# Head gates of a recurrent block from high and low parts in three passes instead of fp32 products

## The reference

```python
def _rg_lru_terms(u, wa, ba, wx, bx, lam):          # u (B,T,1024), wa, wx (8,128,128)
    uh = u.reshape(bsz, n, RG_HEADS, RG_BLOCK)
    r = sigmoid(einsum("bthi,hij->bthj", uh, wa) + ba)
    i = sigmoid(einsum("bthi,hij->bthj", uh, wx) + bx)
    log_a = -RG_C * r * softplus(-lam)
    return exp(log_a), sqrt(-expm1(2.0 * log_a)) * (i * u)

# branches: z = h @ w_in; g, rec = halves of z; u = depthwise conv of 4 taps over rec; gelu(g)
# per direction: context scanned first, latent scan starts from its final state
# out = (gelu(g) * (scan forward + scan backward)) @ w_out
```

## Time and profile before

| | us |
|---|---|
| median of 3 runs (lowest, highest) | 2131.16 (2128.59, 2137.18) |
| the profiled execution | 2134.52 |
| its span | 2132.8 |
| PE, DVE, ACT, POOL busy | 2053.1, 1519.2, 831.5, 1292.4 |
| L752, gate products, records in the span | 192, from 88.9 to 345.2 |
| `u` ready in heads 0, 1, 2 and 7 | 88.9, 125.2, 159.9, 336.4 |

### The profile page before, as it was taken

How to read it: one execution, slowest core, us unless ns; L and a number is a source line. 1 busy time by engine, 2 the same in 40 slices (tenths; PEclk the granted TensorE clock), 3 DMA queues, 4 the chain that set the end, 5 groups by cost and what they waited for, 6 DMA issues and landing times. The chain is left out here.

```text
span 2132.8 us, 26628 instructions
## 1 busy us (share of the span) xinstructions
PE 2053.1 (96%) x9048; PEld 1661.6 (78%) x9048; DVE 1519.2 (71%) x1518; ACT 831.5 (39%) x1111; POOL 1292.4 (61%) x836
## 2 busy tenths in 40 slices
PE   6999999999999999999999999799999999999996
PEld 6677776878888888888888779678888888888885
DVE  7588889878777777777777674696655665566557
ACT  4666667447222232323222355463232223222322
POOL 4533234656877787787778352367765576557653
PEclk9999999999999999999999988899999999999998
DMA  8132322431222222222221400211111111111114
GB/s 306 69 119 71 121 75 88 192 139 60 80 89 89 88 79 89 89 73 86 91 89 65 168 30 11 89 51 68 49 49 49 59 49 49 49 59 49 49 40 158
DMA packets 55932, 179.68 MB, mean 84 GB/s; under 512 B 5041, under 2 KB 6353, under 8 KB 55249
## 3 DMA queue, kind: packets, MB, share of 16 engines
q1 hardware_dynamic: 55888, 179.13, 24.2%
HBM read 166.52 MB, written 12.58 MB: 84 GB/s over the span
## 5 line engine op out<-in xcount | busy, mean ns | idle before, releaser
L2089 DVE TENSOR_TENSOR Y<-Y,ps 128x1024 f32<-128x1024 f32 x336 | 409.9, 1221 | 53.8 <-PE ps L584 13.8
L1693 POOL TENSOR_TENSOR F_lo<-S,F_hi 128x1024 fp32r<-128x1024 f32 x44 | 107.1, 2434 | 351.5 <-ACT F_hi L1354 351.5
L584 PE MATMUL ps<-F_hi,WC_hi 128*128 128x512 f32 x736 | 231.7, 392 | 1.1 <-ACT Y L1392 1.1
L1329 ACT ACTIVATE S<-S 128x1024 f32<-128x1024 f32 x48 | 50.9, 1060 | 464.6 <-DVE S L2193 464.6
L584 PE MATMUL ps<-F_hi,WC_lo 128*128 128x512 f32 x736 | 230.5, 391 | 0.0
L1112 ACT ACTIVATE So_hi<-So_raw 128x512 fp32r<-128x512 f32 x132 | 82.7, 628 | 369.3 <-POOL So_raw L1567 365.7
L584 PE MATMUL ps<-F_lo,WC_hi 128*128 128x512 f32 x704 | 217.4, 390 | 0.0
L1671 POOL TENSOR_TENSOR So_lo<-So_raw,So_hi 128x512 fp32r<-128x512 f32 x132 | 188.4, 1453 | 5.8 <-ACT So_hi L1112 5.8
L584 PEld LDWEIGHTS ps<-F_hi,WC_hi 128*128 128x128 f32 x736 | 138.7, 189 | 31.3 <-ACT Y L1392 1.7
L584 PEld LDWEIGHTS ps<-F_hi,WC_lo 128*128 128x128 f32 x736 | 138.7, 188 | 29.2
L584 PEld LDWEIGHTS ps<-F_lo,WC_hi 128*128 128x128 f32 x704 | 132.4, 188 | 28.1
(11 more groups left out here) (302 smaller groups left out, 5381.1 us busy)
## 6 DMA issues: line engine op xcount, KB each, us to landing
rawA<-wA SPq DMA_DIRECT2D x62, 512.0 KB, 3.3
rawB<-wB SPq DMA_DIRECT2D x62, 512.0 KB, 3.3
E<-ada SPq DMA_DIRECT2D x46, 512.0 KB, 3.3
rawC<-wC SPq DMA_DIRECT2D x46, 512.0 KB, 3.6
quad<-ada SPq DMA_DIRECT2D x8, 2048.0 KB, 9.4
ada_first<-ada SPq DMA_DIRECT2D x4, 2048.0 KB, 16.1
outT<-X SPq DMA_DIRECT2D x16, 512.0 KB, 3.4
X<-outT SPq DMA_DIRECT2D x16, 512.0 KB, 7.0
```

What stands on the lines that cost most here:

```text
L584: mm = pe.matmul(out, w[:, w_cols:w_cols + P], (hi, lo)[part], start=first and w is W_hi[s] and part == 0, stop=last and w is W_lo[s])
L1329: A(S[0][:], S[0][:], ACT.Gelu_apprx_tanh).then_inc(gelu_done, 1)
L1693: TT(dst[:], S[1][:], F_hi[:].bitcast(F32), ALU.subtract).then_inc(f_ready, 1)
L2089: TT(Y[:, m], Y[:, m], flat(ps[:, b:b + 2, :]), ALU.add).then_inc(d_added, 1)
```

## The change

`gw` and `u` are split into high and low parts. ScalarE rounds `u` behind the convolution (`u_hi_ctx`, and the latent tokens into `F_lo`, a tile of a later stage that is free here); GpSimd makes `u_lo_ctx` and `u_lo` from them, and this now stands ahead of WA_lo in its order. ScalarE rounds the next head's `gw` between the next B weights and tanh (`round_gates`); GpSimd makes `gw_lo` as the last of its head. TensorE makes each gate in three passes (low x low is left out) in an order in which the first three passes need no low part of `u`. The load of the next `gw` no longer waits for the gates, but for `gw_lo`. Six semaphores of the context norm become one, with steps (the order of that work stays). `rec` starts 24 bytes later, so that `u_lo_ctx` can lie on it once the convolution has read it.

```diff
-        rec, u, RA0, Hc_hi, Hc_lo, RA1, IB0, IB1, TH0, TH1, gw = overlay(
-            64, ("rec", [P, TA + 3]), ("u", [P, TA]), ("RA0", [P, TA]), 1.25,
+        rec_pad, u, RA0, u_hi_ctx, Hc_hi, Hc_lo, RA1, IB0, IB1, TH0, TH1, gw, gw_hi, gw_lo = overlay(
+            64, ("rec", [P, TA + 9]), ("u", [P, TA]), ("RA0", [P, TA]), ("u_hi_ctx", [P, NC_], F32R), 0.125,
...
+        rec = rec_pad[:, 6:TA + 9]
+        u_lo_ctx, = overlay(64 + 1 / 32, ("u_lo_ctx", [P, NC_], F32R))
@@ SyncE, head_loads
-                    sp_.wait_ge(gate_done, 4 * hd + 4)
+                    sp_.wait_ge(gw_ready, hd + 1)
                     sp_.dma_start(gw[:], gatew[hd + 1]).then_inc(gw_full, 16)
@@ TensorE, head
-                pe.wait_ge(gw_full, 16 * hd + 16)
-                pe.wait_ge(u_made, hd + 1)
-                for gi in range(4):
...
-                    for out, src in ((ps[:, b, 0:NC_], u[:, 0:NC_]), (ps[:, b + 1], u[:, LAT:LAT + HF]),
-                                     (ps[:, b + 2], u[:, LAT + HF:TA])):
-                        mm = pe.matmul(out, gw[:, gi], src, start=True, stop=True)
-                    mm.then_inc(gate_done, 1)
+                pe.wait_ge(gw_ready, hd + 1)
+                pe.wait_ge(u_hi_made, hd + 1)
+
+                def gate_pass(gi, n):
+                    b = 3 * (gi % 2)
+                    w = gw_lo if n == 1 else gw_hi
+                    parts = (u_lo_ctx, u_lo) if n == 2 else (u_hi_ctx, F_lo)
+                    for out, src in ((ps[:, b, 0:NC_], parts[0][:]), (ps[:, b + 1], parts[1][:, 0:HF]),
+                                     (ps[:, b + 2], parts[1][:, HF:T])):
+                        mm = pe.matmul(out, w[:, gi], src, start=n == 0, stop=n == 2)
+                    return mm
+
+                for gi, n in ((0, 0), (0, 1), (1, 0), (0, 2), (1, 1), (1, 2), (2, 0), (2, 1), (2, 2), (3, 0), (3, 1), (3, 2)):
...
+                    if (gi, n) == (0, 2):
+                        pe.wait_ge(u_ready, hd + 1)
+                    if gi > 1 and n == 0:
                         pe.wait_ge(gate_evac, 4 * hd + gi - 1)
+                    mm = gate_pass(gi, n)
+                    if n == 2:
+                        mm.then_inc(gate_done, 1)
@@ ScalarE, head: behind round_hi("A", hd + 1)
+                act.wait_ge(u_made, hd + 1)
+                A(u_hi_ctx[:], u[:, 0:NC_], ACT.Copy)
+                A(F_lo[:], u[:, LAT:TA], ACT.Copy).then_inc(u_hi_made, 1)
@@ ScalarE, head: ahead of tanh
                 round_hi("B", hd + 1)
+                if not last:
+                    round_gates(hd + 1)
...
+            def round_gates(hd):
+                act.wait_ge(gw_full, 16 * hd + 16)
+                if not (isinstance(hd, int) and hd == 0):
+                    act.wait_ge(gate_done, 4 * hd)
+                A(gw_hi[:], gw[:], ACT.Copy).then_inc(gw_hi_made, 1)
@@ GpSimd
+            def lo_of_gates(hd):
+                pool.wait_ge(gw_hi_made, hd + 1)
+                TT(gw_lo[:], gw[:], gw_hi[:].bitcast(F32), ALU.subtract).then_inc(gw_ready, 1)
+
             def head(hd, last=False):
+                pool.wait_ge(u_hi_made, hd + 1)
+                TT(u_lo_ctx[:], u[:, 0:NC_], u_hi_ctx[:].bitcast(F32), ALU.subtract)
+                TT(u_lo[:], u[:, LAT:TA], F_lo[:].bitcast(F32), ALU.subtract).then_inc(u_ready, 1)
                 lo_of_unit("A", hd + 1)
-                pool.wait_ge(u_made, hd + 1)
...
                     lo_of_unit("B", hd + 1)
+                    lo_of_gates(hd + 1)
```

More of the change, by code:

```diff
@@ L98, in build_trunk @@
         W_lo = {"A": sb("WA_lo", [P, D], F32R), "B": sb("WB_lo", [P, D], F32R), "C": WC_lo}
+        u_lo, = overlay(("u_lo", [P, T], F32R))
         S = [sb("S0", [P, T]), S1]
@@ L123, in build_trunk @@
             ("ada_first", [P, ADA0, D]), ("ctx_x", [P, KT, NC_]), ("ctx_sq", [P, KT, NC_]), ("diag_c", [P, 2, P]))
-        rec, u, RA0, Hc_hi, Hc_lo, RA1, IB0, IB1, TH0, TH1, gw = overlay(
-            64, ("rec", [P, TA + 3]), ("u", [P, TA]), ("RA0", [P, TA]), 1.25,
+        rec_pad, u, RA0, u_hi_ctx, Hc_hi, Hc_lo, RA1, IB0, IB1, TH0, TH1, gw, gw_hi, gw_lo = overlay(
+            64, ("rec", [P, TA + 9]), ("u", [P, TA]), ("RA0", [P, TA]), ("u_hi_ctx", [P, NC_], F32R), 0.125,
             ("Hc_hi", [P, KT, NC_], F32R), ("Hc_lo", [P, KT, NC_], F32R), ("RA1", [P, TA]),
-            ("IB0", [P, TA]), ("IB1", [P, TA]), ("TH0", [P, TA]), ("TH1", [P, TA]), ("gw", [P, 4, P]))
+            ("IB0", [P, TA]), ("IB1", [P, TA]), ("TH0", [P, TA]), ("TH1", [P, TA]), ("gw", [P, 4, P]),
+            ("gw_hi", [P, 4, P], F32R), ("gw_lo", [P, 4, P], F32R))
+        rec = rec_pad[:, 6:TA + 9]
+        u_lo_ctx, = overlay(64 + 1 / 32, ("u_lo_ctx", [P, NC_], F32R))
         RA, IB, TH = (RA0, RA1), (IB0, IB1), (TH0, TH1)
@@ L244, in build_trunk @@
         rstd_made, rb_done = ([sem(f"{n}{h}") for h in range(2)] for n in ("rstd_made", "rb_done"))
-        csq_made, cssq_done, crms_made = sem("ctx_sq_made"), sem("ctx_ssq_done"), sem("ctx_rms_made")
-        crstd_made, cdiag_made, crb_done = sem("ctx_rstd_made"), sem("ctx_diag_made"), sem("ctx_rb_done")
+        ctx_step = sem("ctx_step")
+        CTX = {name: n + 1 for n, name in enumerate(("squares", "sum", "columns", "root", "inverse", "diagonal", "spread"))}
+        gw_hi_made, gw_ready, u_hi_made, u_ready = sem("gw_hi"), sem("gw_ready"), sem("u_hi"), sem("u_ready")
         cscaled, caffine, chi, hc_ready = sem("ctx_scaled"), sem("ctx_affine"), sem("ctx_hi"), sem("ctx_h_ready")
@@ L714, in _ @@
             ada_tile(0)
-            pe.wait_ge(csq_made, 2)
+            pe.wait_ge(ctx_step, CTX["sum"])
             for t in range(2):
                 mm = pe.matmul(ps[:, 0, t:t + 1], diag_c[:, t], ones[:, 0:1], start=True, stop=True)
-            mm.then_inc(cssq_done, 1)
+            mm.then_inc(ctx_step, 1)
             for n in range(1, 4):
                 ada_tile(n)
-            pe.wait_ge(cdiag_made, 1)
-            pe.matmul(ps[:, 3, 0:NC_], ones[:], diag_c[:], start=True, stop=True).then_inc(crb_done, 1)
+            pe.wait_ge(ctx_step, CTX["diagonal"])
+            pe.matmul(ps[:, 3, 0:NC_], ones[:], diag_c[:], start=True, stop=True).then_inc(ctx_step, 1)
             part_columns(16, 4, 4, 0)
@@ L739, in head @@
                     unit("B", hd, AB67)
-                pe.wait_ge(gw_full, 16 * hd + 16)
-                pe.wait_ge(u_made, hd + 1)
-                for gi in range(4):
-                    if gi == 0:
+                pe.wait_ge(gw_ready, hd + 1)
[9 more added lines that the diff above has]
+                for gi, n in ((0, 0), (0, 1), (1, 0), (0, 2), (1, 1), (1, 2), (2, 0), (2, 1), (2, 2), (3, 0), (3, 1), (3, 2)):
+                    if (gi, n) == (0, 0):
                         pe.wait_ge(rec_evac, hd + 1)
-                    elif gi == 1:
+                    if (gi, n) == (1, 0):
                         pe.wait_ge(ada_added, hd + 1)
-                    else:
+                    if (gi, n) == (0, 2):
+                        pe.wait_ge(u_ready, hd + 1)
+                    if gi > 1 and n == 0:
                         pe.wait_ge(gate_evac, 4 * hd + gi - 1)
-                    b = 3 * (gi % 2)
-                    for out, src in ((ps[:, b, 0:NC_], u[:, 0:NC_]), (ps[:, b + 1], u[:, LAT:LAT + HF]),
-                                     (ps[:, b + 2], u[:, LAT + HF:TA])):
-                        mm = pe.matmul(out, gw[:, gi], src, start=True, stop=True)
-                    mm.then_inc(gate_done, 1)
+                    mm = gate_pass(gi, n)
+                    if n == 2:
+                        mm.then_inc(gate_done, 1)
                 if not last:
@@ L1159, in _ @@
             act.wait_ge(ctx_full, 16)
-            A(ctx_sq[:], ctx_x[:], ACT.Square).then_inc(csq_made, 1)
+            A(ctx_sq[:], ctx_x[:], ACT.Square).then_inc(ctx_step, 1)
             act.wait_ge(memset_done, 3)
-            act.wait_ge(cssq_done, 1)
-            A(rms_c[:], ps[:, 0, 0:2], ACT.Sqrt, scale=1.0 / D, bias=eps[:, 0:1]).then_inc(crms_made, 1)
+            act.wait_ge(ctx_step, CTX["columns"])
+            A(rms_c[:], ps[:, 0, 0:2], ACT.Sqrt, scale=1.0 / D, bias=eps[:, 0:1]).then_inc(ctx_step, 1)
             for m in range(KT):
@@ L1237, in head @@
                     act.preload_act_table(ACT.Sqrt)
+            def round_gates(hd):
[3 more added lines that the diff above has]
+                A(gw_hi[:], gw[:], ACT.Copy).then_inc(gw_hi_made, 1)
             act.wait_ge(lam_ready, 1)
             act.wait_ge(zeros_ready, 1)
+            round_gates(0)
             head(0)
@@ L1626, in head @@
                     lo_of_unit("B", hd + 1)
-            pool.wait_ge(u_made, 1)
+                    lo_of_gates(hd + 1)
+            lo_of_gates(0)
             head(0)
@@ L1933, in _ @@
             TT(pbs[:], col("pool_b", 0, 8), col("pool_scale", 0, 8), ALU.mult)
-            dve.wait_ge(csq_made, 1)
+            dve.wait_ge(ctx_step, CTX["squares"])
```

(12 more changed lines are left out.)

## The result

| | before | changed |
|---|---|---|
| median (lowest, highest), 5 runs each | 2133.02 (2128.59, 2137.18) | 2152.17 (2148.19, 2158.75) |
| the profiled execution, its span | 2134.52, 2132.8 | 2158.75, 2156.8 |
| ratio to before | | 1.0098, 95% interval 1.0073 to 1.0124 |
| `u` ready, heads 1 to 7 | 125.2, 159.9, 195.2, 230.5, 265.8, 301.1, 336.4 | 126.2, 163.1, 202.6, 242.2, 279.4, 318.9, 358.4 |

The kernel is 19 us slower (16 to 26 by the interval), forecast 18. The profiled execution is the slowest of the five; between the two traces lie 24 us, and all of them come from the heads: +22.1 at the last `u`, +24.7 at the first norm behind them (the reciprocal at 408.6 against 433.4), +24.0 at the last norm of the kernel (2117.6 against 2141.6).

What follows compares the result with a forecast made beforehand. Two rings of almost the same length were taken to close each head, with `u` having about 0.5 us of slack. +12 us at the last `u`, +4.3 last head and +2 clock made +18 on 2131.2: 2149 us, range 2130 to 2163.

Steps and rivals of the forecast that it cites:

- What bounds the loop: Head loop: two dependency cycles of almost the same length close each head, leaving `u` about 0.5 us of slack.
- the two rings: Head-loop cycles from gate products to sqrt: one returns through Gelu and B unit, one through VectorE's scan and convolution.
- Part 1: TensorE's gate products: three passes take 7.0 us for four gates instead of 8.58, 1.6 us less a head.
- Part 2: Rounding and subtraction ahead of the gates: low parts ready at +5.8, last sigmoid at 12.35 instead of 9.66, +2.7 us.
- Part 3: Rounding the gate weights on ScalarE between B's rounding and tanh: +0.5 us, tanh at 15.2.
- Part 4: WA_lo moved from beside the convolution: its first instruction takes 0.95 instead of 2.96 us, -2.0 us every head.
- Part 5: VectorE alternating with GpSimd: `Y*TH` to 18.5, ada quad to 24.95, late by 0.6 us, its idle time gone.
- The sqrt would allow the next product at 24.4: VectorE's next product in a loop head: 21.16 plus 2.7 for sigmoids and 0.5 for gate weights.
- The clock: TensorE's clock drops behind a new 2 to 2.7 us gate stop: one head in four, +2 us, bounds 0 and 10.
- Hand-overs: Switches of the shared read path between GpSimd and VectorE: no price in the rows; at about 115 ns each, 2156.
- Last head: Low parts of the gated tokens behind the last `u`: VectorE comes to them late by the same alternation, +4.3 us.
- the ring: The closed chain of dependent instructions that sets a head's length, gate products through sigmoids, tanh and sqrt back to gate products.

Runs made afterwards that it cites:

- e7: Kernel before with one line moved: GpSimd waits for `u` before WA_lo, gates still fp32; 2134.9 us, ratio 1.0011.
- e1: Changed kernel with the sum of the two scans put into `rec`, so tanh waits for that sum and not `Y*TH`; 2141.98 us, ratio 1.0046.
- e4: Changed kernel with 12 extra 512-column products on TensorE in front of the wait for Gelu, to hold the clock up; 2161.16 us, ratio 1.0135.
- e5: Changed kernel with VectorE instead of GpSimd making the low parts of `u`; 2148.05 us, ratio 1.0074.
- e6: Changed kernel with VectorE making the low parts of `u` and the scans' sum put into `rec`; 2140.74 us, ratio 1.0026.
- e9: Changed kernel: VectorE makes `u`'s low parts, scan sum in `rec`, `Y*TH` behind next head's ada quad, extra weights ahead of head 0; 2133.83 us, ratio 1.0008.
- e8: Changed kernel without the low part of `u` and the third gate pass, scans' sum in `rec`; 2127.11 us, ratio 0.9966.
- e2: Changed kernel without the low part of `u` and the third pass of each gate; 2139.58 us, ratio 1.0033.

## Why the prediction came out right, and where it was wrong

- *What bounds the loop:* right for the kernel before. `u` had next to no slack, and what was put behind it was paid. e7 shows the two rings: 2 us off the convolution alone leave the head at 35.3.
- *Part 1:* the pass rate held (12 passes in the pattern of unit A, 0.58 apart). None of the 1.6 us came back in the changed kernel, and what they are worth when nothing waits is not measured.
- *Part 2:* right to 0.4 us. Low parts +5.4 (5.8 forecast), GpSimd's first piece got in ahead of VectorE's IB product, u_lo 3.25 us in record. Where the low parts hold the gates (e1, heads 2 and 5), the last sigmoid comes at +12.0 (12.35); the +12.5 of the head above agrees by luck, for there the late B unit held them.
- *Part 3:* right, +0.5 and nothing else; tanh at +14.8 in e1 (15.2).
- *Part 4:* the 2.0 us came (0.93 instead of 2.96). That WA_lo costs nothing in its new place was right for TensorE and wrong for VectorE, where part 5 charged it.
- *Part 5:* its times were right: `Y*TH` ended at +18.1 (18.5), the quad at +24.45 (24.95). **The step that failed is "The sqrt would allow the next product at 24.4".** It added the delays of the sigmoids and the weights to tanh and did not ask what else tanh waits for. I had `Y*TH` end at 18.5 and tanh begin at 15.2 in one text, and tanh overwrites what `Y*TH` reads. Before, `Y*TH` ended at 206.43, 0.7 ahead of tanh (207.17): a wait with a cover of 0.7 us, which no view of waits lists. The product came at +27.5, a long head is 39.5 and not 37.05. e1 takes this wait away and lands at 36.41.
- *The clock:* it fell where I put it in one head only. The gates' stop for the low parts was forecast at 2 us and more in each head; it was 1.97 us in head 1 of the changed kernel, and there the clock fell (0.69 from 132 to 134, 0.50 from 134 to 136), with the last sigmoid 0.85 us later than in e1. In later heads the stop was 0.8 us or none, 1.1 in e1. In the four long heads the clock fell behind the 3.7 us in front of the B unit, which follow from the tanh wait. By e4 these falls cost a long head nothing, where I had put in 2 us; the one in head 1 even made the head short (36.98 us against 39.52 in e4), because GpSimd's second IB product (+14.4) came behind `Y*TH` (+14.15).
- *Hand-overs:* right, they have no price in the rows. `Y*TH` ends 1.08 us behind the product that held it up, and takes 1.23 where nothing does (head 1 of the changed kernel).
- *Last head:* +2.6 (24.7 - 22.1) against 4.3.

So 19 against 18 is luck in part. What the prediction described is e1, and e1 loses 8 us by the medians and not 18. By its trace it is 7.3 us at the last `u` (343.7; 12 forecast, in heads of 36.41 and not 37.05) and 3.0 in the last head (4.3), two of which are gone again at the end of the span; the clock stays at 1.00 in all its loop heads (2). The wait that I had missed put 10 to 11 us on top and filled the gap. By the traces the loss is 22.1 + 2.6 = 24.7 against 12 + 4.3 + 2. The sign of the change and the time at which the low parts are ready were understood; about half of the loss came by a wait that the prediction did not have.

## What to carry to other kernels

When an instruction is made late, list every reader of what other instructions are waiting to overwrite, with the cover each wait has today; a wait covered by 0.7 us is in no list of waits and can become the bound first. It happened twice here: tanh behind `Y*TH`, and in e5, e6 and e9 the third sigmoid behind the long scan. Work moved to GpSimd beside VectorE is paid on both engines: count for each of VectorE's instructions with two SBUF inputs whether GpSimd asks first. A faster product is worth what the loop's other engines leave of it (in e8, 1.0 us of 3.2), and an operand that must first be split sits on the ring.

## What the runs showed of the hardware

- Two engines that ask for the shared read path within 0.2 to 0.4 us of each other settle by who asks first, for the whole instruction: 1.23 or 3.79 us for the same TH sum. That is enough to make a loop alternate between two lengths (39.5 and 37.2; 37.4 and 34.8 in e2; 38.8 and 36.4 in e5).
- TensorE's clock fell behind a stop of 1.97 us in head 1 of the changed kernel, and stayed at 1.00 behind a stop of 1.98 us in head 1 of e1, at the same place and behind the same products. It fell also behind 3.7 us, and behind 1.78 us in the kernel before. The length of one stop does not tell, nor does the work just before it. The gates' first low pass and the clock behind it, first in the changed kernel, then in e1 (columns as in the earlier trace rows):

```profile
131.64 0.39 PE L754 MATMUL ps<-u_lo_ctx,gw_hi 128*128 128x256 f32 x1 [1.97 <-POOL u_lo L1650]
```

```profile
132.00:134.00 2.00, 2.00 (x9) 1.35 (x7) 1.97 (x2) 1.28 (x2) 2.00 (x1) 0.69 0.00 0
134.00:136.00 2.00, 2.00 (x6) 1.56 (x6) 2.00 (x1) 1.67 (x3) 0.31 (x2) 0.50 0.30 35
```

```profile
130.72 0.38 PE L754 MATMUL ps<-u_lo_ctx,gw_hi 128*128 128x256 f32 x1 [1.98 <-POOL u_lo L1652]
```

```profile
130.00:134.00 4.00, 2.69 (x12) 2.00 (x13) 3.96 (x2) 2.20 (x4) 3.39 (x2) 1.00 0.00 0
```
